# Seven of the eleven gate-and-up chunks in each feed-forward read their 512 moving columns in another order, or take the two row tiles in turn

## What is computed

```python
D_MODEL = 1024
SEQ = 256
D_FF = 2816

def swiglu_ffn(h, w_gate, w_up, w_down):
    return (jax.nn.silu(h @ w_gate) * (h @ w_up)) @ w_down

for l in range(DEPTH):                    # block one; block two has one such line per layer
    h = rms_norm(x, norm_pre[l, 0])
    x = x + 0.5 * rms_norm(swiglu_ffn(h, ffn1_w_gate[l], ffn1_w_up[l], ffn1_w_down[l]), norm_post[l, 0])
```

## Time and profile before

| | |
|---|---|
| median of 2 runs | 2031.38 us (2031.17 to 2031.59) |
| span of the profiled execution | 2030.4 us |
| instructions | 24123 |
| TensorE matmul, busy | 2010.3 us (99% of the span), 9514 matmuls |
| VectorE busy | 1443.8 us (71%) |
| ScalarE busy | 1120.8 us (55%) |
| granted TensorE clock, mean | 1.000 |
| matmuls on line 622 | 8112 recorded |

### The profile page before, as it was taken

How to read it: one execution, slowest core, us unless ns; L and a number is a source line. 1 busy time by engine, 2 the same in 40 slices (tenths; PEclk the granted TensorE clock), 3 DMA queues, 4 the chain that set the end, 5 groups by cost and what they waited for, 6 DMA issues and landing times.

```text
span 2030.4 us, 24123 instructions
## 1 busy us (share of the span) xinstructions
PE 2010.3 (99%) x9514; PEld 1653.6 (81%) x9514; DVE 1443.8 (71%) x1915; ACT 1120.8 (55%) x1414; POOL 0.2 (0%) x4
## 2 busy tenths in 40 slices
PE   8999999999999999999999999999999999999998
PEld 7888887888888888887888888888888888888887
DVE  6666899776667566999776567966665669667565
ACT  6445667564445455667564446656644457566443
POOL 0000000000000000000000000000000000000000
PEclk9999999999999999999999999999999999999999
DMA  8776764557766775664567767554676675546774
GB/s 262 231 209 176 238 187 145 187 185 214 210 207 222 231 213 176 219 187 147 185 187 222 203 184 222 177 168 139 188 216 205 189 204 186 170 152 187 209 214 122
DMA packets 351410, 394.54 MB, mean 194 GB/s; under 512 B 123825, under 2 KB 259649, under 8 KB 351297
## 3 DMA queue, kind: packets, MB, share of 16 engines
q1 hardware_dynamic: 347200, 381.94, 62.2%
q10 hardware_dynamic: 4096, 11.05, 1.6%
HBM read 365.66 MB, written 1.05 MB: 181 GB/s over the span
## 4 chain that ended last, share of the span: by engine, by line
PE 90%; DVE 5%; ACT 2%; DMA 2%; issue 1%; SPq 0%; ACTq 0%; DVEq 0%
PE ps L622 83%; DVE w_lo L1875 1%; PE ps L693 1%; DVE scratch L2154 1%; PE ps L1204 1%; PE ps L1185 1%; DVE x L1925 0%; ACT w_hi L1264 0%; DMA raw<-in_w_in 0%; DMA raw<-in_w_co 0%; DVE scratch L2191 0%; PE ps L716 0%; DVE scratch L2067 0%; DMA x<-in_x 0%; PE ps L1068 0%
## 5 line engine op out<-in xcount | busy, mean ns | idle before, releaser
L1875 DVE TENSOR_TENSOR w_lo<-raw,w_hi 128x2048 fp32r<-128x2048 f32 x336 | 767.8, 2289 | 217.6 <-ACT w_hi L1264 214.4
L1264 ACT ACTIVATE w_hi<-raw 128x2048 fp32r<-128x2048 f32 (+2 forms) x340 | 644.2, 1897 | 469.0 <-PE ps L622 232.6
L622 PE MATMUL ps<-w_hi,hT_hi 128*128 128x512 f32 x2048 | 806.1, 394 | 0.0
L622 PE MATMUL ps<-w_lo,hT_hi 128*128 128x512 f32 x2048 | 798.2, 390 | 0.0
L622 PE MATMUL ps<-w_hi,hT_lo 128*128 128x512 f32 x2048 | 774.0, 389 | 0.0
L622 PEld LDWEIGHTS ps<-w_hi,hT_hi 128*128 128x128 f32 x2048 | 385.1, 188 | 83.0 <-issue 5.5
L622 PEld LDWEIGHTS ps<-w_hi,hT_lo 128*128 128x128 f32 x2048 | 384.4, 188 | 80.8
L622 PEld LDWEIGHTS ps<-w_lo,hT_hi 128*128 128x128 f32 x2048 | 385.1, 188 | 77.0
L622 PE MATMUL ps<-w_hi,bT_hi 128*128 128x512 f32 x656 | 257.7, 393 | 0.0
L622 PE MATMUL ps<-w_lo,bT_hi 128*128 128x512 f32 x656 | 255.4, 389 | 0.0
L622 PE MATMUL ps<-w_hi,bT_lo 128*128 128x512 f32 x656 | 255.4, 389 | 0.0
(11 more groups left out here) (294 smaller groups left out, 1124.2 us busy)
## 6 DMA issues: line engine op xcount, KB each, us to landing
raw<-in_w_in SPq DMA_DIRECT2D x160, 512.0 KB, 4.6
raw<-in_ffn_w_down SPq DMA_DIRECT2D x88, 512.0 KB, 4.3
raw<-in_ffn_w_gate SPq DMA_DIRECT2D x86, 512.0 KB, 4.0
raw<-in_ffn_w_up SPq DMA_DIRECT2D x86, 512.0 KB, 5.0
raw<-in_w_gate SPq DMA_DIRECT2D x44, 512.0 KB, 4.0
raw<-in_w_up SPq DMA_DIRECT2D x44, 512.0 KB, 5.0
raw<-in_w_down SPq DMA_DIRECT2D x44, 512.0 KB, 4.3
raw<-in_w_out SPq DMA_DIRECT2D x32, 512.0 KB, 4.2
```

The source lines that it names most:

```text
L622: mm = nc.tensor.matmul(bank(t, half), act[:, tiles[i], t * P:(t + 1) * P], w, start=start and (i, n) == steps[0], stop=stop and (i, n) == ...
L1264: nc.scalar.activation(dst, src, ACT.Copy).then_inc(high_ready, 1)
L1875: V.tensor_tensor(lo, src, flat(hi), ALU.subtract).then_inc(low_ready, 1)
```

## The change

Inside the loop over chunks, each of the chunks 2 to 8 gets an entry of a list `orders`. Six entries permute the 512 columns of a matmul, the same way in the moving operand and in the output bank, so every value still lands in its own column. With `("even_odd", n)` the columns are cut into blocks of n, and all even blocks are read first, then all odd ones; with `("halves", n)` a block of n comes from the first 256 columns, then one from the second 256, and so on. n is 32, 16 or 2. The seventh entry, `"alternate"`, leaves the columns alone and makes the row tile the inner loop, so that the two row tiles (and their banks 6 and 7) take turns. Chunks 0, 1, 9 and 10, every `down` and everything outside the feed-forwards stay as they are. The numbers of instructions, semaphores and transfers stay the same, on all engines.

```diff
+        def columns(w, order):
+            if order is None:
+                return w
+            kind, n = order
+            if kind == "even_odd":
+                return w.rearrange("p (b e n) -> p e b n", e=2, n=n)
+            return w.rearrange("p (h b n) -> p b h n", h=2, n=n)
+
         def products(left, tiles, parts, bank, start, stop, before=None, halves=1, mark=None, before_low=None,
-                     rows=range(TT)):
+                     rows=range(TT), order=None):
...
+            if order == "alternate":
+                for i, n in steps:
+                    act, part = passes[n]
+                    for t in rows:
+                        mm = nc.tensor.matmul(bank(t, 0), act[:, tiles[i], t * P:(t + 1) * P], parts[part][:, i, :],
+                                              start=start and (i, n) == steps[0], stop=stop and (i, n) == steps[-1])
+                return mm
...
-                        mm = nc.tensor.matmul(bank(t, half), act[:, tiles[i], t * P:(t + 1) * P], w,
+                        mm = nc.tensor.matmul(columns(bank(t, half), order), act[:, tiles[i], t * P:(t + 1) * P],
+                                              columns(w, order),
                                               start=start and (i, n) == steps[0], stop=stop and (i, n) == steps[-1])
...
+            orders = [("even_odd", 32), ("even_odd", 16), ("even_odd", 2), ("halves", 32), ("halves", 16), ("halves", 2), "alternate"]
+
             def gate_up(M, k, c, bank=mid):
                 if bank is mid:
                     pe.wait_ge(hid_ready, f * NCHUNK + c)
+                order = orders[c - 2] if 2 <= c < 9 else None
                 for kh in range(2):
-                    square(M, k + kh, hT, 4 * kh, bank, kh == 0, kh == 1)
+                    square(M, k + kh, hT, 4 * kh, bank, kh == 0, kh == 1, order=order)
```

More of the change, by code:

```diff
@@ L642, in left_ready, with square @@
             return first(lambda t: pe.wait_ge(hT_ready, L.sub(j, 4, 2 * t + kh + 1)))
-        def square(L, k, left, first, bank, start, stop, before=None, mark=None):
+        def square(L, k, left, first, bank, start, stop, before=None, mark=None, order=None):
             weights(L, k)
             products(left, range(first, first + 4), split(L, k, by4), bank, start, stop, before, 1,
-                     mark).then_inc(unit_done, 1)
+                     mark, order=order).then_inc(unit_done, 1)
         def first_pair(L, j, k, second, banks, bank_free=lambda t: None):
```

## The result

The changed kernel takes 2143.99 us (median of 2 runs, 2143.48 to 2144.50) against 2031.38 us before: ratio 1.0553, 95% interval 1.0522 to 1.0583.

A forecast was written before the change was run, and what follows sets the result against it. TensorE's matmuls, busy 99% of 2030.4 us, were taken as the bound. Runs of 2 add 122.9 us and the other orders 0, giving 2153.3 us, or 2154 us (+6.0%) with 1.0 us outside the span; range 2028 to 2168 us.

The forecast's parts named there:

- Row tiles in turn: Chunk 8, 288 matmuls: changing the bank after every matmul instead of every twelfth was put at cost 0.
- Runs of 32 and 16: Chunks 2, 3, 5, 6, 1152 matmuls: extra breaks taken as 0; with 1 ns each it would be 26 us.
- The bf16 row: Trace row of 256-column bf16 matmuls in two runs of 128: pace 0.11 to 0.12 us, read as breaks costing nothing.
- Runs of 2: Chunks 4 and 7, 576 matmuls: half of each four-column access thrown away, 426.7 ns instead of 213.3, +122.9 us.
- the upper variant: Chunks 4 and 7: the 13.3 ns double too, so 576 x 226.7 ns = +130.6 us.
- rival (b): Chunks 4 and 7: only one of the two kinds of pairs halves the rate, +61.4 us, 2093 us; chance 0.06.
- theory T: From the experiments, moving operand: even and odd places of the order are fetched by two streams, 1.77 ns per line visit.
- Rival (a): Chunks 2 to 8: pairs are free, so all seven entries cost nothing, 2031 us; chance 0.31.
- (c): All six permuted orders: each break costs up to 1 ns, 173 us, 2205 us; chance 0.07, shared with pairs below half rate.
- The 13.3 ns as a price per matmul: Line 622: 226.7 ns for 512 columns read as 213.3 ns streaming plus 13.3 ns fixed per matmul, also in bf16.
- The 384-column row: Trace row of 384 moving columns, 0.18 us to the next start: 173 fits, 170 fits a little worse.
- Rival (d): Permuted chunks: the 13.3 ns come from reading side by side and other orders lose them, 23 us less, 2008 us; chance 0.02.

The follow-up runs named there:

- the shifted kernel: Changed kernel with only the moving operand altered in chunks 2 to 8, its columns starting 2 or 1 columns off, output written side by side: 2279.73 us.
- the kernel with cut matmuls: Kernel before the change, columns side by side, but each matmul in chunks 2 to 5 cut in two (256/256, 320/192, 384/128, 448/64), taking turns: 2087.52 us.

## Why the prediction was right, and where its sizes were off

**Bound.** That only TensorE's pace counts was right: no other engine's busy time moved by more than 0.5 us, and chunk stretches alone make up 111.0 of 111.3 us.

**Row tiles in turn: 0.** Measured 226.7 ns, so 0.

**Runs of 32 and 16: taken as 0.** They cost 9.8 to 13.3 ns a matmul, 13.4 us in all, inside the bound of 26 us. (The "7 to 31 more breaks" are 15 to 31, as the sum has them.) The bf16 row with one break says nothing of it: its runs are of 128 columns, and runs of 64 and 128 are free here too. Why whole lines cost anything when broken up stays open.

**Runs of 2: taken as +122.9 us.** Measured 288 x (226.2 + 112.9) ns = 97.7 us. The mechanism, half of each access thrown away, was right for the hop of 4, and the shifted kernel shows the unit. Two sizes were off. At a hop of 4 the whole 226.7 ns doubled, as in the upper variant (+130.6 us for both kinds). At a hop of 256 the excess is half as large, 113 ns; rival (b) had foreseen that the two kinds might differ, but put one at nothing. This is the mis-sized term: 65.1 + 32.5 us in place of 61.4 + 61.4. Why the hop of 256 loses only half as much is open; theory T doesn't give it either. Rival (a), pairs free, is refuted; so is (c), since cost doesn't grow with breaks: 127 of them (runs of 4 at a hop of 8) cost 4.3 ns, 31 (runs of 16) 13.3.

**How near the sum came was partly luck.** Against the forecast the first kind of pairs took 3.7 us more, the second 28.9 less, and the runs of 32 and 16, put at nothing, 13.4 more. The errors partly cancel: 2153.3 + 3.7 - 28.9 + 13.4 = 2141.5 us, and the span is 2141.7.

**The 13.3 ns as a price per matmul.** This step failed. With the same matmuls and the same weight loads, another order of columns takes 215.8 ns, so 10.9 of the 13.3 ns belong to the fetch; and in the kernel with cut matmuls 64 columns take 29.2 ns in all, where 13.3 ns for each matmul would make it 40. The 384-column row was too coarse: 0.18 us doesn't tell 170 from 173. The bf16 row does show 0.12 us, but that is also where the 256-column halves of the cut kernel settle after a first one of 113 ns, so it may be the pace of something else; no run tells. The row of 114 ns for 256 columns, which I set aside for its 32 stationary columns, fits theory T: 64 visits x 1.77 = 113 ns. Rival (d) had the cause of the excess right, for orders that the change doesn't have: none of its seven loses the excess. The sum survived because both readings share the doubling.

The Trainium skill's rule in "SBUF — State Buffer", section "Specifications (TRN2)", that a 16-byte line wants at least two uses, taken by itself made pairs free, and they are not (452.9 and 339.6 ns). It agrees with the 452.9 ns if it is applied to every second column of the order, as in theory T: the two columns of a pair belong to different streams, and so give one use each. For the 339.6 ns it doesn't. The measured step of 1.77 ns a visit is near the 1.76 ns that the Trainium skill's "Vector Engine (DVE) Microarchitecture Reference", section "Measured stream behaviour on trn2", gives for a column on VectorE when both sources hop with every element; that the two have one cause is a guess, and no run here tests it. The rule of the Trainium skill's "PSUM — Partial Sum Buffer", section "Specifications (TRN2)", that any non-contiguous pattern slows matmuls significantly, didn't bite: a bank written in runs of 2, 16 or 32 columns cost 0 (226.7 ns).

## What to carry to other kernels

If matmuls of 32-bit reduced columns run unbroken at 227 ns for 512 columns, 11 of these ns are the fetch of the moving operand, and another order can save them: let neighbouring places of the order come from two different lines (one column of the gate, one of the up weight), write the bank side by side, and let the readers of the bank take every second column, which cost them nothing. Runs of fewer than four aligned columns that are not interleaved like that cost 113 to 261 ns a matmul here. Before a small excess over the ideal time is put down to a fixed cost, vary what it could be proportional to, and read single steps, not only the average of a stretch.

## What the hardware showed that I had not expected

An order of columns that looks worse can be faster: 215.8 ns against 226.7 side by side, for every block size tried (4, 8, 16, 32, 64 and 256). A shift of the whole moving operand by 8 bytes doubles runs of 4 (231 to 454 ns) and costs 6 ns even side by side. Runs of 4 vary with the hop by more than the gain in question (223.8, 231, 246.5, 250.2 and 277.9 ns at hops of 16, 8, 32, 256 and 64), for a reason that is open, and the same order of runs of 4 took 223.3, 226.7 and 233.3 ns in different feed-forwards of one kernel. And a step of 2 columns is free for ScalarE and VectorE where they read a bank, but costs them 31% and 16% where they read, and VectorE also writes, SBUF.
